# Second attention's queries and keys stored by residue of the token number modulo 4

## What is computed

```python
q = apply_partial_rope(q, cos, sin); k = apply_partial_rope(k, cos, sin)
for g, (window, dil) in enumerate(DILATED_GROUPS):
    # heads of group g; tokens split by residue modulo dil
    o, lse = banded_window_attention(to_residue(q), to_residue(k), to_residue(v), window // dil)
alpha = softmax(lse over the three groups)
mixed = sum over groups of alpha * o
```

## Time and profile before

| | |
|---|---|
| three executions | 1919.22, 1924.22, 1926.08 us |
| the profiled execution's own time | 1924.52 us |
| its span, first to last instruction | 1922.7 us |
| PE busy | 1837.8 us, 96% of the span |
| DVE busy | 983.0 us, 51% |
| ACT busy | 654.5 us, 34% |
| second attention (last values included) | 1319.8 to 1490 us of the span |
| granted TensorE clock, mean | 0.983 |

### The profile page before, as it was taken

The page is one execution under the profiler, slowest core; times in us unless marked ns, Lnnn a source line. Parts: engine busy times, 40 slices in busy tenths (PEclk is TensorE's granted clock), DMA queues, the critical chain, the costliest instruction groups (busy, mean ns, idle before and its releaser), DMA issues.

```text
span 1922.7 us, 22773 instructions
## 1 busy us (share of the span) xinstructions
PE 1837.8 (96%) x9403; PEld 1333.5 (69%) x9403; DVE 983.0 (51%) x1620; ACT 654.5 (34%) x1126; POOL 85.1 (4%) x70
## 2 busy tenths in 40 slices
PE   6999999999999699999999989999999999999998
PEld 4877887788878434344343258889787878888886
DVE  5888887842553413132222244545775666536643
ACT  4455445542342302011010033423656433222233
POOL 0200001000000000000000000002130200000000
PEclk9999999999999799999999999999999999999999
DMA  9332423253343399999999963244213322242221
GB/s 324 133 121 88 132 88 99 93 192 103 102 167 140 127 374 421 421 421 421 421 421 421 422 215 124 72 142 128 86 46 108 132 88 71 92 134 88 74 91 44
DMA packets 174521, 355.10 MB, mean 185 GB/s; under 512 B 7154, under 2 KB 144466, under 8 KB 149074
## 3 DMA queue, kind: packets, MB, share of 16 engines
q1 hardware_dynamic: 170672, 338.85, 47.9%
q10 hardware_dynamic: 3458, 14.50, 2.1%
q0 software_dynamic: 288, 0.30, 0.1%
HBM read 345.53 MB, written 8.39 MB: 184 GB/s over the span
## 4 chain that ended last, share of the span: by engine, by line
PE 81%; DVE 9%; DMA 4%; ACT 3%; issue 2%; POOL 1%; SPq 0%; ACTq 0%; DVEq 0%
PE ps L497 78%; PE ps L500 3%; DMA rx<-in_w_exp_down 1%; DMA rx<-in_w_exp_gate 1%; POOL X L2822 1%; DVE wsq1l L1905 1%; DMA md<-in_w_mod 1%; DVE k2l L1905 1%; DVE wsp0l L1905 1%; DVE X L1914 1%; DVE small L2150 1%; DVE wsq0l L1905 1%; ACT M L1260 1%; ACT KR L1260 0%; DVE tb L1905 0%
## 5 line engine op out<-in xcount | busy, mean ns | idle before, releaser
L497 PE MATMUL ps<-H,wsq1h 128*128 128x512 f32 x640 | 198.8, 392 | 3.2 <-DVE H L1914 2.0
L497 PE MATMUL ps<-H,wsq0h 128*128 128x512 f32 x608 | 189.4, 393 | 0.0
L497 PE MATMUL ps<-rx,XE 128*64 128x512 f32 x752 | 178.6, 606 | 2.8 <-DMA rx<-in_w_exp_up 2.2
L497 PE MATMUL ps<-H,wsp1h 128*128 128x512 f32 x544 | 172.6, 399 | 1.4 <-DVE wsp1l L1905 1.4
L497 PEld LDWEIGHTS ps<-H,wsq1h 128*128 128x128 f32 x640 | 119.1, 188 | 28.4 <-issue 4.1
L497 PEld LDWEIGHTS ps<-H,wsq0h 128*128 128x128 f32 x608 | 113.4, 188 | 24.6 <-issue 1.7
L497 PE MATMUL ps<-H,wsq1l 128*128 128x512 f32 x320 | 124.7, 390 | 0.0
L497 PE MATMUL ps<-H,wsp0h 128*128 128x512 f32 x368 | 121.6, 408 | 2.1 <-ACT H L1260 2.1
L1905 DVE TENSOR_TENSOR wsq1l<-ring,wsq1h 128x1024 fp32r<-128x1024 f32 (+2 forms) x72 | 83.0, 1191 | 75.7 <-ACT wsq1h L1260 75.7
L497 PE MATMUL ps<-H,wsq0l 128*128 128x512 f32 x304 | 118.5, 390 | 0.0
L497 PEld LDWEIGHTS ps<-rx,XE 128*64 128x64 f32 x752 | 49.8, 138 | 95.7 <-issue 84.7
(11 more groups left out here) (378 smaller groups left out, 3499.5 us busy)
## 6 DMA issues: line engine op xcount, KB each, us to landing
rx<-in_w_exp_gate SPq DMA_DIRECT2D x49, 1024.0 KB, 17.4
rx<-in_w_exp_down SPq DMA_DIRECT2D x46, 1024.0 KB, 20.9
rx<-in_w_exp_up SPq DMA_DIRECT2D x45, 1024.0 KB, 19.3
ring<-in_w_in SPq DMA_DIRECT2D x37, 1024.0 KB, 5.4
ring<-in_w_up SPq DMA_DIRECT2D x20, 1024.0 KB, 5.1
ring<-in_w_exp_up SPq DMA_DIRECT2D x19, 1024.0 KB, 20.8
ring<-in_w_mod SPq DMA_DIRECT2D x18, 1024.0 KB, 6.9
ring<-in_w_exp_down SPq DMA_DIRECT2D x18, 1024.0 KB, 19.2
```

The costliest lines, as they stand in the source:

```text
L497: return pe.e.matmul(o, l, r, start=start, stop=stop, skip_group_check=True)
```

## The change

The three tiles keep their size, but queries of all groups, and keys of groups 1 and 2, are stored with the tokens of one residue modulo 4 side by side: [r][j] for token 4j + r. Keys of group 0 stay in natural order. The copies that write the tiles read their sources (`u`, and `leading` on VectorE) with a step of four fp32 values and write contiguously; `scores2` reads contiguous runs of 128. The number of instructions, waits and transfers is the same.

```diff
+    q2r, k2hr, k2lr = (x[:, :].rearrange("p (g i r j) -> p g i r j", g=3, i=2, r=4) for x in (q2, k2h, k2l))
+
+    def by_residue(x):
+        return x.rearrange("p (j r) -> p r j", r=4)
...
-                    qa = q2v[:, g, i, r:T:4]
+                    qa = q2r[:, g, i, r, :]
...
-                        mm(S1, qa, k2hv[:, g, i, r:T:4], True, False)
-                        mm(S1, qa, k2lv[:, g, i, r:T:4], False, False)
+                        mm(S1, qa, k2hr[:, g, i, r, :], True, False)
+                        mm(S1, qa, k2lr[:, g, i, r, :], False, False)
...
-                        t = act(k2hv[half, g, i, :], u[r, :], ACT.Copy)
+                        if g:
+                            t = act(k2hr[half, g, i, :, :], by_residue(u[r, :]), ACT.Copy)
+                        else:
+                            t = act(k2hv[half, g, i, :], u[r, :], ACT.Copy)
                 else:
-                    t = act(q2v[0:64, g, i, :], u[r, :], ACT.Copy, scale=0.125)
+                    t = act(q2r[0:64, g, i, :, :], by_residue(u[r, :]), ACT.Copy, scale=0.125)
...
-                        t = tt(k2lv[half, g, i, :], u[r, :], leading[r, :].bitcast(F32), ALU.subtract)
+                        if g:
+                            t = tt(k2lr[half, g, i, :, :], by_residue(u[r, :]), by_residue(leading[r, :].bitcast(F32)),
+                                   ALU.subtract)
+                        else:
+                            t = tt(k2lv[half, g, i, :], u[r, :], leading[r, :].bitcast(F32), ALU.subtract)
                 else:
-                    t = stt(q2v[64:128, g, i, :], u[r, :], 0.125, leading[r, :].bitcast(F32), ALU.mult, ALU.subtract)
+                    t = stt(q2r[64:128, g, i, :, :], by_residue(u[r, :]), 0.125, by_residue(leading[r, :].bitcast(F32)),
+                            ALU.mult, ALU.subtract)
```

## The result

Twenty executions of the changed kernel gave a median of 1926.63 us (1921.29 to 1934.33), twenty of the one before beside them 1921.81. The ratio is 1.0025, with a 95% interval of 1.0014 to 1.0036: 4.8 us slower (2.7 to 6.9), within the half per cent that counts as no change. The forecast was a sum of +3.2 us.

What follows compares the result with a forecast made beforehand. PE alone was taken to bound the score rounds, with DVE's chain ending last where queries and keys are made. Gain -7.0 plus copies +10.2 gave +3.2 us on 1924.52, stated as 1927.5 us, range 1917 to 1937.

Steps and rivals of the forecast that it cites:

- Two rules: Second attention: time taken from scores counts fully only in rounds 1 to 3 (six of eight); DVE copy time in both jj.
- The gain of 7.0 us: PE's scores with contiguous reads: 1.16 us less per round, six rounds 7.0 us, bounds 2.7 to 9.3.
- 0.24 to 0.27 are the strided loads, one after another: PE's small triples: the queries' strided weight loads set these times; contiguous, a triple takes 0.29 us instead of 0.565.
- DVE's copies, 5.1 us per jj: DVE's stepped copies lengthen each jj's chain: keys 3.1 plus queries 1.95 us; 10.2 us for two jj.
- 0.39 us from `hT<-tb,cst`: Added price of each stepped `k2l` on DVE, from a row with one stepped source: 1079 ns against 684.
- ACT at nothing: ACT's stepped copies, keys' four 2.1 us and queries' two 1.0 us added, are covered and cost 0.
- just used up: ACT's 1.00 us idle ahead of `tbr` is filled by the 1.0 us its two query copies add.
- The clock plays no part: TensorE's granted clock is 1.00 in these stretches, at the 2.4 GHz level, so no cost was counted.
- The predicted wait of 1 to 2 us for `pp`: PE's waits for `pp`, behind its wait for the third group's `k2l`, become 1 to 2 us.
- Dear copies: Rival: two stepped sources on DVE paid separately, chains 11 us longer per jj; +15 us, 1939.5 us; chance 0.2.
- free ones: Rival: DVE's copies cost almost nothing, chains grow 0 to 2 us each; 7 to 9 us gained, about 1917.5; chance 0.2.
- Small matmuls that stay at 0.21 to 0.24 us: Rival: PE's 128-column matmuls stay so despite contiguous weights; 2.7 - 10.2 gives +7.5 us, 1932; chance 0.1.

Runs made afterwards that it cites:

- e3_reads: Changed kernel with its copies put back to natural order, only the scores reading contiguous runs (wrong tokens): 1915.16 us, ratio 0.9964 to the kernel before.
- e4_copies: Changed kernel with its reads undone: copies store by residue, scores read with step four (wrong tokens): 1932.70 us, ratio 1.0051.
- e1_queries: Changed kernel with the keys' copies and reads undone, so only the queries are stored by residue: 1921.17 us, ratio 0.9999.
- e2_keys: Changed kernel with the queries' copies and reads undone, so only keys of groups 1 and 2 are stored by residue: 1929.85 us, ratio 1.0034.
- e6_prices: Changed kernel with one source of `k2l` stepped in g = 1, only outputs of `k2l` and `k2h` stepped in g = 2 (wrong tokens): 1927.51 us, one execution.
- e7_fill: Changed kernel plus unused bf16 matmuls (8 in jj 0, 16 in jj 1) where PE waits for the last keys: 1926.6 us, ratio 1.0017.
- e9_psum: Queries alone by residue, the step moved to DVE's cosine product reading PSUM, copies contiguous (wrong tokens' angles): 1916.45 us, one execution.
- e10_tables: Changed kernel's storage, but DVE's shuffle and product read PSUM stepped, with cosine and sine reordered once and contiguous copies: 1918.49 us, ratio 0.9976.
- e8_act: Queries alone by residue, through one stepped ACT copy ahead of its rounding; later query copies contiguous, keys as before: 1917.74 us, ratio 0.9979.
- e5_pool: Queries alone by residue as in e1_queries, the step moved to POOL's add so ACT and DVE copy contiguously: 1921.86 us, ratio 0.9991.

## Why the prediction was right, point by point

**Two rules: scores count in rounds 1 to 3, copies count in both jj.** Right. e3_reads gains nothing in A and C, where round 0 lies, and e4_copies pays in both.

**The gain of 7.0 us.** Measured 6.67 in the change, 6.55 in e3_reads. The second small triple is at the predicted 0.29 us. Two sizes were off and nearly cancelled: the small triple behind group 0's takes 0.41, and group 0's takes 0.59 where 0.66 was taken. A head of 1.29 us gives 2 x (1.83 - 1.29) = 1.08 per round where 1.16 was predicted. The step "0.24 to 0.27 are the strided loads, one after another" held in the main: e1_queries, loads alone, has 2.66 of the 3.27 per jj. But the reading of the earlier trace rows, that stepped keys cost nothing, failed by 0.6 us per jj: e1_queries lacks it and e2_keys has it. The total came near all the same, because the price was taken from whole triples and the change removes both steps.

**DVE's copies, 5.1 us per jj.** Measured 5.17 in jj 0 (43.26 us from first shuffle to the end of the third `k2l`, before 38.09) and 5.07 in jj 1 (38.01 and 32.94). The choice of 0.39 us from `hT<-tb,cst` for two stepped sources was right (four take 4.28 us against 2.79, 0.37 each), and e6_prices shows why the dear case was wrong: the instruction pays once. The `q` pair takes 3.90 us against 3.04, 0.86 more where 0.78 was taken. These small misses go in opposite directions and nearly cancel, which is luck; the mechanism is the one predicted.

The trace agrees here with the Trainium skill, Vector Engine (DVE) Microarchitecture Reference, Measured stream behaviour on trn2: by its 1.76 ns per column for two hopping sources against 1.054, a `k2l` was estimated at 0.36 us more, and 0.37 was measured. The 2.50 ns that the page has for a step of 24 words did not appear with this step of four.

**ACT at nothing.** Right. Its stepped copies of queries take 1.12 us each, 0.48 more than a contiguous one at 2.54 / 4, close to the 0.51 taken; yet ahead of `tbr` ACT still waits for POOL:

```profile
1356.99 0.63 ACT L1266 ACTIVATE tbr<-X 128x512 fp32r<-128x512 f32 x1 [0.43 <-POOL X L2836]
```

The prediction had the cover "just used up". There was 0.43 left, since POOL's add beside DVE's stepped `q` took 2.10 us instead of 1.62, which no step of the prediction had.

**The clock plays no part.** This step failed, and its cost is the larger part of what is left of the sum. The changed kernel makes PE wait 3.21 us in jj 1; then the granted clock is 0.72 and 0.59 in the two windows shown, while before it was 1.00 there. DVE's timeline:

```profile
1450.20 0.68 DVE L1914 TENSOR_TENSOR X<-ps,tb 128x512 f32<-128x512 f32 x1
...
1454.46 0.69 DVE L1914 TENSOR_TENSOR X<-ps,tb 128x512 f32<-128x512 f32 x1 [1.66 <-PE ps L503]
```

C is 5.91 us longer and its chain only 5.07: 0.84 us more, of which D gives 0.12 back, so the clock cost 0.72. In e7_fill, at full clock, C is longer by its chain and no more. The predicted wait of 1 to 2 us for `pp` is there in jj 0 (1.78) and missing in jj 1, because there PE, at the lower clock, was the last to come. In jj 0 it fell too (0.62 from 1352 to 1356, after the 1.73 us wait), at no cost, since DVE was the bound there. The prediction saw that PE would wait and priced the wait itself; it did not ask what PE is like after a wait.

**Sum.** Forecast -7.0 + 10.2 = +3.2; measured -6.55 + 10.24 + 0.72 = +4.41 in the stretch (the 0.12 of D counted with the clock). The gain was 0.45 too high and the clock's 0.7 was missing.

**Rivals.** Dear copies (+15) fell with 1.07 us per `k2l`, free ones (-7) with it too: their gain of 7 us is what the reads alone give, 1915.16 in e3_reads beside 1922.10 for the kernel before. Small matmuls that stay at 0.21 to 0.24 us fell with the 0.12 us between the starts at 1388.57 and 1388.69. Only the first small `k2h` behind group 0 still takes 0.25 us to the next start (1388.32 to 1388.57); why is not shown.

## What to carry to other kernels

When a layout is changed to please one engine, the cost of writing it is paid where the bound engine makes it, so look back along the chain for an instruction that has to run anyway and can take the step free, or for an engine with idle time; here a shuffle and a product that read PSUM took it for nothing, and a change of +4.4 us became one of -6.5. Price a new wait of TensorE twice, once for its length and once for the slower clock behind it, and ask which engine is the bound there.

## What the runs showed of the hardware that was not expected

- A step of four fp32 values costs DVE about 0.38 us per 512 values on SBUF operands of two-source instructions, whether on one source, both, or the output (e6_prices), and nothing where the stepped source is in PSUM: product 686 ns and 685 ns, shuffle 735 ns (e9_psum, e10_tables), as for contiguous PSUM sources in the kernel before (686 and 735 ns). In both kernels only the PSUM bank is read with the step; the other source and the output are contiguous.
- DVE's plain copy with one stepped SBUF source and a contiguous output took 618 ns for 128x512 (e10_tables); I had expected about 1.1 us. No run has the same copy with a contiguous source.
- ACT pays about as much: 1.12 us for a copy of 64x512 with a stepped source, 4.47 us for four with a stepped output, 1.15 for 128x512 (e8_act).
- POOL's add is slower with a step too (3.01 us against 2.14 in e5_pool), and DVE's slab beside it lost the same 0.87 us; beside DVE's stepped `q` pair POOL's contiguous add took 2.10 instead of 1.62.
- All six waits of PE of over 2 us in these stretches (3.21 in the change, 3.20 in e6_prices, 3.21 and 3.26 in e4_copies, 2.58 and 2.10 in e2_keys) were followed by a granted clock of 0.50 or 0.51; of those of 1.4 to 1.8 us some were (1.73 at 1350.67 in the change) and more were not. What tells the latter apart stays open. The fall cost 0.7 us in the change, 0.9 in jj 0 of e4_copies and 1.5 in e1_queries, and nothing in jj 0 of the change and in jj 1 of e4_copies.
